# Moving the weight splits and some attention steps of a hand-laid order on one TensorE-bound core

## The reference

```
log_beta = jax.nn.log_sigmoid(z)
log_one_minus = jnp.where(past, log_beta - z, 0.0)
later = lax.cumsum(log_one_minus, axis=3, reverse=True) - log_one_minus
w = jnp.where(past, jnp.exp(log_beta + later), 0.0)
```

## Time and profile before

| what | value |
|---|---|
| median of three runs | 829.42 us |
| the profiled execution | 832.22 us |
| its span, first to last instruction | 830.40 us |
| mean granted TensorE clock | 0.992 of full speed |
| busy PE / DVE / ACT / POOL | 801.1 / 497.0 / 468.1 / 135.7 us |
| share of PE in the chain that ended last | 86% |
| DMA, share of 16 engines' span | 50.7% |

### The profile page before, as it was taken

How to read it: one execution, slowest core, us unless ns; L and a number is a source line. 1 busy time by engine, 2 the same in 40 slices (tenths; PEclk the granted TensorE clock), 3 DMA queues, 4 the chain that set the end, 5 groups by cost and what they waited for, 6 DMA issues and landing times.

```text
span 830.4 us, 12691 instructions
## 1 busy us (share of the span) xinstructions
PE 801.1 (96%) x4238; PEld 651.2 (78%) x4238; DVE 497.0 (60%) x731; ACT 468.1 (56%) x1004; POOL 135.7 (16%) x204
## 2 busy tenths in 40 slices
PE   7999999999999998899999999999999999999996
PEld 5877778887678885787878887777887888888885
DVE  5455565684565556757765676666787544555454
ACT  6667486475665655555665565564557443444352
POOL 2011021000233110534532545000000000000000
PEclk9999999999999999999999999999999999999999
DMA  8964553469673646533223444457774645566641
GB/s 243 280 163 130 158 172 102 151 193 291 215 216 105 215 136 210 159 102 89 78 84 103 127 121 153 127 178 221 243 243 154 203 152 178 155 194 200 204 135 51
DMA packets 147294, 137.78 MB, mean 166 GB/s; under 512 B 15024, under 2 KB 115648, under 8 KB 147232
## 3 DMA queue, kind: packets, MB, share of 16 engines
q1 hardware_dynamic: 145136, 129.89, 50.7%
q0 software_dynamic: 2096, 7.09, 3.3%
HBM read 135.90 MB, written 1.05 MB: 165 GB/s over the span
## 4 chain that ended last, share of the span: by engine, by line
PE 86%; DVE 4%; ACT 4%; issue 3%; DMA 2%; POOL 1%; SPq 0%; ACTq 0%; DVEq 0%; POOLq 0%
PE psum L1195 67%; PE psum L1173 7%; PE psum L1294 4%; PE psum L1429 3%; DVE w_lo L1672 1%; ACT w_hi L1476 1%; PE psum L1215 1%; PE psum L1355 1%; DMA meta_w<-in_w_in 1%; PE psum L1397 1%; ACT probs L1603 1%; DMA gain<-in_norm_g 1%; DVE probs L1815 1%; POOL rtmp L1141 1%; PE psum L1432 0%
## 5 line engine op out<-in xcount | busy, mean ns | idle before, releaser
L1672 DVE TENSOR_TENSOR w_lo<-raw,w_hi 128x1024 fp32r<-128x1024 f32 (+1 forms) x234 | 273.5, 1185 | 63.0 <-ACT w_hi L1476 30.4
L1195 PE MATMUL psum<-w_hi,h_hi 128*128 128x512 f32 (+1 forms) x656 | 259.6, 396 | 4.4 <-DVE h_lo L1730 1.9
L1476 ACT ACTIVATE w_hi<-raw 128x1024 fp32r<-128x1024 f32 (+1 forms) x234 | 231.1, 1011 | 47.2 <-PE psum L1195 16.8
L1195 PE MATMUL psum<-w_lo,h_hi 128*128 128x512 f32 (+1 forms) x656 | 246.8, 376 | 0.0
L1195 PE MATMUL psum<-w_hi,h_lo 128*128 128x512 f32 (+1 forms) x656 | 246.2, 375 | 0.0
L1195 PEld LDWEIGHTS psum<-w_hi,h_hi 128*128 128x128 f32 x656 | 123.8, 189 | 32.4 <-issue 16.4
L1195 PEld LDWEIGHTS psum<-w_lo,h_hi 128*128 128x128 f32 x656 | 123.5, 188 | 19.1
L1195 PEld LDWEIGHTS psum<-w_hi,h_lo 128*128 128x128 f32 x656 | 124.0, 189 | 15.4
L1195 PE MATMUL psum<-w_hi,m_hi 128*128 128x512 f32 x152 | 60.4, 397 | 1.2 <-DVE m_lo L1730 1.2
L1195 PE MATMUL psum<-w_lo,m_hi 128*128 128x512 f32 x152 | 59.3, 390 | 0.0
L1195 PE MATMUL psum<-w_hi,m_lo 128*128 128x512 f32 x152 | 59.2, 389 | 0.0
(11 more groups left out here) (171 smaller groups left out, 1001.6 us busy)
## 6 DMA issues: line engine op xcount, KB each, us to landing
raw<-in_w_in SPq DMA_DIRECT2D x112, 256.0 KB, 3.6
raw<-in_w_ffn_in SPq DMA_DIRECT2D x88, 256.0 KB, 4.0
raw<-in_w_in SPq DMA_DIRECT2D x24, 512.0 KB, 3.9
raw<-in_w_out SPq DMA_DIRECT2D x24, 512.0 KB, 4.0
raw<-in_w_in SPq DMA_DIRECT2D x64, 192.0 KB, 2.7
raw<-in_w_ffn_out SPq DMA_DIRECT2D x22, 512.0 KB, 3.9
meta_w<-in_w_in SPq DMA_DIRECT2D x10, 1024.0 KB, 7.5
raw<-in_w_mem_kv SPq DMA_DIRECT2D x8, 512.0 KB, 3.7
```

The source lines that it names most:

```text
L1195: last = nc.tensor.matmul(psum[:, bank, 0:n], sx[name][:, c, t * P:(t + 1) * P], wx[:, kk, 0:n], start=u["first"] and kk == 0 and z == 0, ...
L1476: nc.scalar.activation(weights(u)[0][:, :, 0:n], raw[:, u["raw"], :, 0:n], ACT.Copy)\
L1672: nc.vector.tensor_tensor(lo[:, :, 0:n], raw[:, u["raw"], :, 0:n], hi[:, :, 0:n].bitcast(F32), ALU.subtract)\
```

## The change: split places by kind of group, other marks, one split held back

Three things change, all of them in the order of steps; no instruction of arithmetic is added or taken away.

1. **Places of the splits.** `SPLIT_LAST` is replaced by `HI_LAST`, the kinds in which a high split comes behind the steps that are due, and `LO_BEHIND`, how far the low split stands behind: 0 (the default) directly behind its high split, 1 behind the steps that are due, 2 one half unit later. So `mb` and `wo` get the high split first and the low one after the due steps, `diff` the high one first and the low one a half unit later, `mem`, `mkv`, gates, FFN and all others high and low back to back ahead of the evacuation, `sb` and `bswa` both behind the due steps, and `swa` the high one last.
2. **Marks.** Many steps move by a half unit or trade places within one (`SLOTS`).
3. **The last turns.** `fout` units are held after the second, so that one high and low split and the table load come behind `turn_f` instead of ahead of it.

The waits `free_of` and `sums_free` state for the new order which reader frees `probs` and the sums in `stats`; the wait on `probs` moves from `scores` to `soft`.

```diff
-SPLIT_LAST = ("diff", "mb", "wo", "bswa", "mkv")
+HI_LAST = ("bswa", "swa", "sb")
+LO_BEHIND = {"mb": 1, "swa": 1, "diff": 2, "wo": 1}
...
-    "sb": dict(turn_qk=(1,), gate=(1.25, 2.25), scores=(3, 3), later=(4, 4.5), out=(7.75, 7.5),
-               turn_mix=(9,)),
+    "sb": dict(turn_qk=(1,), gate=(1.25, 2.25), scores=(3, 3.5), later=(4.05, 4.05), out=(7.75, 7.5),
+               turn_mix=(8.25,)),
...
-    "diff": dict(turn_qk=(1.5, 2.5), scores=(4.25, 4.25), soft=(4.75, 4.75), blend=(6.25,), turn_p=(7.75,), out=(8.75,),
-                 turn_mix=(9.75,)),
+    "diff": dict(turn_qk=(2, 2.25), scores=(4.75, 5), soft=(6, 6), blend=(6.25,), turn_p=(7.75,), out=(8.75,),
+                 turn_mix=(10.5,)),
...
-        if g["kind"] not in SPLIT_LAST:
+        behind = LO_BEHIND.get(g["kind"], 0)
+        if g["kind"] not in HI_LAST:
             splits()
+            if behind == 0:
+                low_parts(0)
...
-        if g["kind"] in SPLIT_LAST:
+        if g["kind"] in HI_LAST:
+            if behind == 1:
+                low_parts(0)
+            splits()
+            if behind == 0:
+                low_parts(0)
+        elif behind == 1:
             low_parts(0)
-            splits()
-        else:
-            low_parts(0)
+        elif behind == 2:
+            low_parts(len(lows) - late)
...
-    line.append(("tables", None))
     held = outs_of(nf - 3) + outs_of(nf - 2)
-    line.extend(("unit_a", u) for u in held[:3])
-    line.append(("turn_f", dict(j=nf - 1, f=last_g)))
-    line.append(("unit_a", held[3]))
+    line.extend(("unit_a", u) for u in held[:2])
+    line.extend([("hold", "begun"), ("unit_a", held[2]), ("turn_f", dict(j=nf - 1, f=last_g))])
+    line.extend([("hold", None), ("splits", "one"), ("tables", None), ("unit_a", held[3])])
...
+                        wait(act, s["sums_free"])
```

More of the change, by code:

```diff
@@ L146 @@
 SLOTS = {
-    "sb": dict(turn_qk=(1,), gate=(1.25, 2.25), scores=(3, 3), later=(4, 4.5), out=(7.75, 7.5),
-               turn_mix=(9,)),
-    "mb": dict(turn_qk=(2.5,), gate=(2.25, 4.25), scores=(3, 3), soft=(3.5, 3.5), turn_p=(4.5, 5), out=(5.5, 7),
-               turn_mix=(7.5,)),
-    "mem": dict(turn_qk=(1,), gate=(0.25, 2.25), scores=(1.75, 1.75, 4.25, 4.25), soft=(2.25, 2.25, 4.75, 4.75),
-                turn_p=(4, 5.25, 6.5, 7.5),
-                out=(5.75, 6.75, 7.75, 8.75), turn_mix=(9.75,)),
-    "swa": dict(turn_qk=(3.25, 2.75), scores=(4.45, 4.45, 6.45, 6.45), soft=(4.95, 4.95, 6.95, 6.95),
-                scale=(5.95, 7.95), turn_p=(6.5, 6.5, 8.5, 8.5), turn_tm=(6.9, 8.9), out_t=(7.5, 9.5),
+    "sb": dict(turn_qk=(1,), gate=(1.25, 2.25), scores=(3, 3.5), later=(4.05, 4.05), out=(7.75, 7.5),
+               turn_mix=(8.25,)),
+    "mb": dict(turn_qk=(2.2,), gate=(2.25, 4.25), scores=(3.05, 3.05), soft=(3.5, 3.5), turn_p=(4.5, 5.25),
+               out=(5.5, 6.5), turn_mix=(7.5,)),
+    "mem": dict(turn_qk=(1,), gate=(1.5, 2.25), scores=(1.75, 1.75, 4.25, 4.25), soft=(2.25, 2.25, 4.75, 4.75),
+                turn_p=(4.5, 5.25, 6.5, 7.5), out=(5.75, 7.25, 7.75, 7.75), turn_mix=(9.75,)),
+    "swa": dict(turn_qk=(3.25, 2.75), scores=(3.95, 4.45, 6.45, 6.45), soft=(4.95, 4.95, 6.95, 6.95),
+                scale=(5.7, 7.95), turn_p=(6.5, 6.5, 8, 8.5), turn_tm=(6.95, 8.9), out_t=(7.75, 9.5),
                 mix_t=(7.95, 9.95)),
-    "diff": dict(turn_qk=(1.5, 2.5), scores=(4.25, 4.25), soft=(4.75, 4.75), blend=(6.25,), turn_p=(7.75,), out=(8.75,),
-                 turn_mix=(9.75,)),
+    "diff": dict(turn_qk=(2, 2.25), scores=(4.75, 5), soft=(6, 6), blend=(6.25,), turn_p=(7.75,), out=(8.75,),
+                 turn_mix=(10.5,)),
 }
@@ L232, in part @@
                 low_parts(len(lows) - 1 - lows.index(u))
+        late = len(lows)
         steps.append((name, u))
@@ L298, in number @@
     probs_reader = {}
+    sums_reader = {}
+    kinds = {}
     outs_of_pt = []
@@ L315, in ring, with free_of @@
         ring_free.append(free)
+    def free_of(readers, j):
+        if j % 4 not in readers:
+            return None
+        of, signal = readers[j % 4]
+        assert of == j - 4 or (readers is sums_reader and kinds[j - 4] not in ("mb", "mem"))
+        return signal
     for what, s in steps:
@@ L367, in number @@
             s["j"] = j = pl.next("jobs") - 1
-            s["p_free"] = probs_reader.get(j % 4)
+            kinds[j] = g["kind"]
             s["meta_out"] = meta_turned.get(j % 2)
@@ L371, in number @@
                 s["sb"] = pl.next("sbs") - 1
+                s["p_free"] = free_of(probs_reader, j)
             else:
@@ L376, in number @@
             g["last_scores"] = j + 1
+        elif what == "soft":
+            s["p_free"], s["sums_free"] = free_of(probs_reader, s["j"]), free_of(sums_reader, s["j"])
         elif what == "turn_qk":
@@ L390, in number @@
             s["blended"] = pl.next("blends")
-            probs_reader[(s["j"] + 1) % 4] = ("blended", s["blended"])
+            probs_reader[(s["j"] + 1) % 4] = (s["j"] + 1, ("blended", s["blended"]))
         elif what == "turn_p":
@@ L415, in number @@
             g["last_out"] = s["o"] + 1
+            assert s["heads"][0]["pt"] == len(outs_of_pt)
             outs_of_pt.extend([s["o"] + 1] * 2)
```

9 lines of the change are left out of this document (6 added, 3 removed).

## The result

The kernel after takes 812.91 us, the median of four runs (812.42 to 813.14). The ratio to the kernel before, measured beside it, is 0.977 (95% interval 0.9747 to 0.9795); in two later sets of runs it was 0.976 (0.9737 to 0.9789) and 0.977 (0.9747 to 0.9796). The direction was right. The gain was not 13.0 us but 16.5 against the median that the forecast started from, and 19 by the ratio.

The account below looks back on a forecast made before the run. PE, busy 801.1 of 830.4 us, was taken as the bound, so only its waits and switches could move: 13.8 + 0.9 - 1.7 = 13.0 us off the 829.4 median gives 816.4, range 812.5 to 819.5 (0.70).

Parts of the forecast that it names:

- First layer: First layer: three PE waits would go, 4.1 us with the correction; 0.2 us off for the very first pair.
- Windowed: Windowed groups: five PE waits would go as low splits move behind the division, 2.4 us.
- Into the differential groups and in them: Differential groups: one wait for `out_t` on the way in (1.5 us) and five for the blend (3.4 us) would go.
- FFN start and last turns: FFN start: one wait gone, 0.4 us; last turns: `m_hi` starts earlier, 1.4 us less 0.4 for a late low split.
- correction of 0.16 per wait: PE's waits: each costs about 0.16 us more than its idle time, 2.9 us over 18 waits.
- New waits, 1.7 off: Half a dozen places with under 0.5 us to spare: 1.7 us taken off the gain, bounds 0 and 7.
- thin places: Places with under 0.5 us to spare: `p_tm`, the bank ahead of the blended turn, pieces of the memory's turn.
- Switches, 0.9: PE's returns to the units: 22 fewer (186 to 164) would save 0.9 us, bounds 0 and 2.4.
- POOL's wait, "unchanged": PE's wait for the rotary on POOL: 1.8 us, said to stay because the change leaves its step in place.
- Half comes back: Rival: PE's small steps wait for PSUM banks, or low splits hold up the rotary; 822.4 us, chance 0.17.
- Late scores: Rival, differential groups: `scores` start 2.2 us later and PE waits in 8 groups; 836 us, chance 0.08 (slower).
- No change: Rival: PE's waits are only pushed on to the next join, the last turns alone gain; 828.4 us, chance 0.05.

Follow-up runs that it names:

- no_diff: The kernel after with the marks of the differential row put back as before; median 819.5 us, ratio to the kernel before 0.9841.
- mix_alone: The kernel after with the turn of the mix of the differential groups a half unit later, standing alone; median 813.7 us, ratio to before 0.9777.
- no_first: The kernel after with the marks of the first two layers (`sb`, `mb`, `mem`) as before; median 815.1 us, ratio to before 0.9789.
- before_behind_rope: The kernel before with one added DVE wait for POOL's first windowed rotation ahead of a low split; median 827.9 us, ratio to before 0.9953.

## Why the prediction was right, and where it failed

The mechanism was right: the waits that the forecast counted went, for the reasons it gave. It failed in size, by terms that it put at nothing or wrong: the clock (0; the runs show 3.0), new waits (1.7 taken off; nothing net), the returns (0.9; some 1.9), three delays in the gates (0; 0.8) and POOL's wait ("unchanged"; 0.6 shorter).

**What bounds the kernel.** Right. PE's idle time fell to 17.7 us.

**Waits.** First layer 4.1 less 0.2: 4.1 measured. Windowed 2.4: 2.4, and besides 0.57 at the first differential `turn_qk`, which the profile put down to "issue" and which I had seen and not counted. Into the differential groups and in them 4.9: 4.9; five blends and `out_t`, with their 0.16 for the modelled ends, as the earlier trace rows gave them. `bswa` 1.2: 1.25. FFN start and last turns 0.4 and 1.0: 0.44 and 1.10, to which the table's row adds the new `o_st` and leaves out the 0.28 that stays at the last turns. The correction of 0.16 per wait was needed: it is 2.9 of PE's 7.6 us of busy time.

**New waits, 1.7 off.** The first step that failed. What is new by the trace is 0.40 (`o_st` in the FFN), 0.28 (`out_t`) and 0.28 (a turn of the normed memory), 1.0 in all. The last two are among the thin places that the prediction named, the first is not; the other thin places held. As much went that was not counted (0.57, and 0.36 at a `turn_qk` of the first layer). Net nothing, where the sum held 1.7. That the two sides cancel is luck; the lump was too large by 0.7 for what is new, and had nothing on the other side.

**Switches, 0.9.** Mis-sized. Outside the places with a changed clock, what the table does not count as a wait fell by 2.2 us. Of that, 0.8 are the three delays in the gates, which are waits that the forecast did not see, and the two new ones of 0.28 go the other way; so 2.16 - 0.82 + 0.56 = 1.9 is left for the 22 fewer returns. The bounds were 0 and 2.4, and I took a value near the lower one, on the thought that neighbouring small steps cost something between themselves. The runs price a net return at 0.11 (no_diff) and 0.12 (mix_alone) in the differential groups and 0.06 (no_first) in the first two layers; 11 x 0.11 + 14 x 0.06, less 0.3 for three returns more in the windowed groups, is 1.7.

**POOL's wait, "unchanged".** The step that failed in kind. The prediction said that the change leaves POOL's wait where it is. It named the rule that would have told otherwise, and applied it to the blend only; for low splits against the rotation it took nothing, and listed it as a rival with a loss. The change moves a low split behind the turn that waits for POOL, and so takes it out of POOL's last copy: 0.6 us, in the trace stem from. That this wait can be 1.2 or 2.0 with the same places could not be known from one trace, but four instances of one copy, two of 0.90 and 0.98 us beside two of 0.29, were there to be read.

**Clock.** Not in the sum at all, though the table ahead of the prediction has 0.992; it is the largest term that was missed, 3.0 us over all executions. Three falls of the clock lay in the span of the profiled execution of before (from 8, 329 and 353 us) besides one at its end, and one (from 328) in that of after besides the end. The change takes away the wait of 1.7 us at 73 and shortens that of 1.8 at 352, behind which falls were seen. before_behind_rope shows it for the second; that the first has a part in the 3.0 is argued from one trace. The start is chance: in the three traces of the kernel after that stretch takes 0.98 and 0.15 us less and 0.06 more than in the first trace of before.

**Base.** The forecast went from 829.4, the median of three. In 66 executions the median is 832.1. Against 829.4 the gain was 16.5, which by coincidence is the change in time x clock; the forecast for that was 13.0. The sum closes to about half a microsecond: 13.8 for the waits, nothing net for new ones, 0.8 for the gates, 1.9 for the returns and 0.6 for POOL's copy make 17.1, against 16.5 in time x clock and 16.8 at equal clock. The prediction also gives two upper ends, 819.5 in the chances and 823.5 below them; neither matters here, as the miss is at the other end.

**Rivals.** Half comes back: refuted; 1.0 of new waits came, and as much went that had not been counted. Late scores: they come late and cost nothing, while with the old marks (no_diff) they come earlier and the blend is 0.45 late. That what stood on DVE and PE between the two had been the cost is the likely reading; no run moves those steps alone. The rotations of the differential groups are held by low splits, as that rival said, but nobody waits for them. No change: refuted; ACT and DVE had the room.

## What to carry to other kernels

When PE is the bound, count three things apart: the waits, the returns to the long run of matmuls (0.06 to 0.12 us each here), and the clock behind long waits. Here a wait of some 2 us was in part of the executions followed by a lower clock that cost 1.6 us more, so the longest single waits are worth more than their length. Look also below the resolution of the list of waits: three delays of 0.27 us in an unbroken run of matmuls were 0.8 us. Look at instructions of one form whose durations differ between instances (0.86 and 4.39, 0.29 and 1.10): they tell of a hold between engines that no list of waits names, and moving one instruction may lift it. And take several executions before you fix a base: three were 2.7 us off the median of 66.

## What the hardware showed that I had not expected

A queue of DVE subtractions with two SBUF inputs keeps a POOL instruction out until the last of them is done: 4.39 us for four, 2.67 for two, 5.58 for four and two short ones, in each case the sum of their lengths and 0.86. Fills on DVE let it pass.

The granted clock fell to its lower level behind PE waits of 1.7 us or more in some executions and not in others of the same kernel (behind the wait for POOL in two of four traces with the old places, behind that for `m_lo` in one of four), so that one kernel takes 828.4 or 834.5 us with nothing else changed.
